# Experts in pairs: both down-projections side by side, one combine per pair

## The reference

```
logits = t @ w_router + b_router            # 288 x 32 experts
top_v, top_e = lax.top_k(logits, 4); gates = softmax(top_v)
# for every expert e, for the tokens that chose it:
hh = xb @ w1[e] + b1[e]                     # 1024 -> 2048
glu, lin = split(hh); glu = min(glu, 7); lin = clip(lin, -7, 7)
act = glu * sigmoid(1.702 * glu) * (lin + 1)
out = act @ w2[e] + b2[e]                   # 1024 -> 1024
y += gate * out                             # back to each token's row
```

## Time and profile before

| | us |
|---|---|
| median of 3 runs | 1418.36 (1416.41 to 1418.98) |
| profiled execution, span (all that the page gives of it) | 1417.7 |
| TensorE matmuls busy | 1293.6 (91%) |
| TensorE weight loads busy (beside the matmuls) | 632.8 |
| VectorE busy | 508.9 (36%) |
| ScalarE busy | 202.4 (14%) |
| GpSimd busy | 138.0 (10%) |
| up-projections, line 1601 | 452.0 |
| down-projections, line 1631 | 226.8 |
| combines, line 1577 | 196.2 |
| gathers, line 1557 | 74.1 |
| read from memory | 460.84 MB |

### The profile page before, as it was taken

How to read it: one execution, slowest core, us unless ns; L and a number is a source line. 1 busy time by engine, 2 the same in 40 slices (tenths; PEclk the granted TensorE clock), 3 DMA queues, 4 the chain that set the end, 5 groups by cost and what they waited for, 6 DMA issues and landing times.

```text
span 1417.7 us, 18156 instructions
## 1 busy us (share of the span) xinstructions
PE 1293.6 (91%) x6994; PEld 632.8 (45%) x6994; DVE 508.9 (36%) x907; ACT 202.4 (14%) x354; POOL 138.0 (10%) x100
## 2 busy tenths in 40 slices
PE   5999997869499999999999999999999999999995
PEld 4788897748232433333333333333333333333341
DVE  3455888546623132222223132222222232222313
ACT  2332011010310111101011111111110111111012
POOL 6102266611300000000000000000000000000000
PEclk9999998979699999999999999999999999999998
DMA  9632386684689999999999999999999999999940
GB/s 316 199 121 76 119 268 209 226 329 176 243 350 413 386 398 398 393 402 385 415 385 416 382 398 398 383 414 384 413 388 411 387 405 389 386 406 392 417 169 35
DMA packets 123892, 467.05 MB, mean 329 GB/s; under 512 B 7440, under 2 KB 54064, under 8 KB 90864
## 3 DMA queue, kind: packets, MB, share of 16 engines
q1 hardware_dynamic: 116848, 455.37, 81.6%
q0 software_dynamic: 1616, 6.65, 1.5%
q10 hardware_dynamic: 5392, 4.54, 1.0%
HBM read 460.84 MB, written 5.70 MB: 329 GB/s over the span
## 4 chain that ended last, share of the span: by engine, by line
PE 84%; DVE 10%; ACT 2%; issue 2%; DMA 2%; DVEq 0%; SPq 0%; ACTq 0%
PE bank L1601 31%; PE bank L1631 16%; PE bank L1577 11%; PE bank L1256 8%; PE bank L1557 5%; PE bank L1420 4%; PE bank L1408 2%; PE bank L1619 1%; DVE rest L978 1%; ACT rest L719 1%; DVE split L931 1%; DMA ring<-w_in 1%; PE bank L1595 1%; DVE rest L1174 1%; DVE rest L1002 1%
## 5 line engine op out<-in xcount | busy, mean ns | idle before, releaser
L1601 PE MATMUL bank<-ring,rest 128*64 128x512 f32 x2048 | 452.0, 594 | 0.0
L1174 DVE TENSOR_TENSOR rest<-rest,bank 128x512 f32<-128x512 f32 (+1 forms) x198 | 133.8, 682 | 498.4 <-PE bank L1577 498.3
L1601 PEld LDWEIGHTS bank<-ring,rest 128*64 128x64 f32 x2048 | 144.3, 137 | 286.9 <-issue 281.2
L1631 PE MATMUL bank<-ring,rest 128*64 128x512 f32 x1024 | 226.8, 595 | 11.1 <-ACT rest L719 11.1
L1577 PE MATMUL bank<-rest 128*128 128x512 f32 (+1 forms) x396 | 196.2, 617 | 24.8 <-DVE rest L1174 23.7
L1256 PE MATMUL bank<-rest,ring 128*128 128x288 f32 (+1 forms) x512 | 125.2, 405 | 16.2 <-DMA ring<-w_in 16.2
L1631 PEld LDWEIGHTS bank<-ring,rest 128*64 128x64 f32 x1024 | 70.7, 137 | 146.6 <-issue 127.9
L1577 PEld LDWEIGHTS bank<-rest 128*128 128x128 f32 (+1 forms) x396 | 51.3, 161 | 166.4 <-DVE rest L1174 97.5
L1256 PEld LDWEIGHTS bank<-rest,ring 128*128 128x128 f32 x512 | 98.0, 193 | 40.9 <-DMA ring<-w_in 16.2
L715 ACT ACTIVATE rest<-rest 128x512 f32<-128x512 f32 x32 | 20.1, 630 | 575.1 <-DVE rest L1192 575.1
L1420 PE MATMUL bank<-split 128*128 128x288 f32 x576 | 86.8, 314 | 10.2 <-DVE split L980 5.7
(11 more groups left out here) (296 smaller groups left out, 779.2 us busy)
## 6 DMA issues: line engine op xcount, KB each, us to landing
ring<-w SPq DMA_DIRECT2D x384, 1024.0 KB, 8.4
ring<-w_in SPq DMA_DIRECT2D x12, 1024.0 KB, 13.4
ring<-k_t SPq DMA_DIRECT2D x8, 1024.0 KB, 5.4
ring<-v_c SPq DMA_DIRECT2D x8, 1024.0 KB, 12.8
ring<-w_xk SPq DMA_DIRECT2D x4, 1024.0 KB, 5.1
ring<-w_xv SPq DMA_DIRECT2D x4, 1024.0 KB, 5.1
ring<-w_out SPq DMA_DIRECT2D x4, 1024.0 KB, 5.9
ring<-w_xq SPq DMA_DIRECT2D x4, 1024.0 KB, 5.8
```

What stands on the lines that cost most here:

```text
L1174: v.tensor_tensor(dst, dst, ps[6 + q % 2][0:R, :], ALU.add).then_inc(comb_free, 1)
L1601: last = t.matmul(out, slots[:, k, :], w[:, col], start=False, stop=(k == KT - 1))
L1631: last = t.matmul(ps[2 + ds][CAP * cg:CAP * cg + CAP, :], actT[:, a * P + CAP * cg:a * P + CAP * cg + CAP], w[:, cg, 512 * ds:512 * ds + 5 ...
```

## The change

Experts are worked in pairs, and the loop's body is two pairs instead of four experts. The code changes in five places.
- A pair's units come as 8 of the first expert's `w1`, 8 of the second's, then the 8 of `w2` in turn from both.
- TensorE does the first up-projection, with the previous pair's combine after unit 3, then the second, with the first expert's transposes after unit 4, then the gather for the next pair, the second expert's transposes and both down-projections. In these the upper 64 partitions of a bank belong to the first expert and the lower to the second, and each half adds up the whole sum over 1024.
- One combine serves a pair: slots 0 to 63 are the first expert's, 64 to 127 the second's.
- The slot weights are no longer built per tile and transposed. The gates are split into three bf16 parts and transposed once, ahead of the loop (`gate_rows`, 96 rows), and the places likewise (`place_rows`). Two bf16 matmuls per pair copy the rows of the two experts to 64 partitions each (banks 6 and 7); ScalarE copies the gates to SBUF, and one VectorE operation writes the gate where the place is the slot's number (`slot_no`).
- The first combine now has 96 rows: three gate parts, with `b2` loaded three times.

```diff
-            q -= W1_UNITS
+            if q < 2 * W1_UNITS:
+                e, q = e + q // W1_UNITS, q % W1_UNITS
...
+            e, q = e + q % 2, (q - 2 * W1_UNITS) // 2
...
 # ScalarE, per pair
+                    act_e.wait_ge(actt_ps, 2 * n + 1)
+                    a.copy(actT[0], ps[4][:, :]).then_inc(actt_done, 1)
+                    act_e.wait_ge(bcast_ps, n + 1)
+                    a.copy(gate_b, ps[6][:, 0:T]).then_inc(gate_copied, 1)
...
+                    evac_gather(n + 2, (j + 1) % 2)
+                    act_e.wait_ge(actt_ps, 2 * n + 2)
+                    a.copy(actT[1], ps[6][:, :]).then_inc(actt_done, 1)
...
 # VectorE, ahead of the loop
+            link(v.tensor_copy(g_part, gates))
+            link(v.tensor_copy(gates3[:, :, 0, :], g_part))
+            link(v.tensor_tensor(g_rest, gates, gates3[:, :, 0, :], ALU.subtract))
...
 # VectorE, per pair
+                    pick_pair(e + 2, (j + 1) % 2)
+                    dve.wait_ge(xg_ps, 2 * n + 2)
+                    select_pair(e + 2)
+                    add_combined(n + r)
+                    activate(2 * n, n * PAIR_UNITS + W1_UNITS, 2 * j)
+                    dve.wait_ge(bcast_ps, n + 1)
+                    dve.wait_ge(gate_copied, n + 1)
+                    v.scalar_tensor_tensor(selGT[:, 0:T], ps[7][:, 0:T], slot_no, gate_b,
+                                           ALU.is_equal, ALU.mult).then_inc(selgt_done, 1)
+                    activate(2 * n + 1, n * PAIR_UNITS + 2 * W1_UNITS, 2 - 2 * j)
...
 # TensorE, per pair
+                    up_bias(1)
+                    for k in range(KT):
+                        up(1, k)
+                        if k == 4:
+                            pe.wait_ge(act_done, 2 * n + 1)
+                            turned(4)
...
+                            t.matmul(ps[6][:, 0:T], oh[j][0:96, :], gate_rows[0:96], start=True, stop=True)
+                            t.matmul(ps[7][:, 0:T], oh[j][0:96, :], place_rows[0:96], start=True, stop=True).then_inc(bcast_ps, 1)
+                    pe.wait_ge(sel_done, n + 2)
+                    pe.wait_ge(actt_done, 2 * n + 1)
+                    gather()
+                    pe.wait_ge(act_done, 2 * n + 2)
+                    pe.wait_ge(selgt_done, n + r + 2)
+                    turned(6)
+                    pe.wait_ge(actt_done, 2 * n + 2)
+                    for q in range(W2_UNITS):
...
+                                for x in range(2):
+                                    last = t.matmul(ps[2 * j + ds][CAP * x:CAP * x + CAP, :],
+                                                    actT[x][:, q * P + CAP * h:q * P + CAP * h + CAP],
+                                                    w[x][:, h, 512 * ds:512 * ds + 512],
+                                                    start=(q == 0 and h == 0), stop=(q == W2_UNITS - 1 and h == 1))
```

More of the change, by code:

```diff
@@ L123, in hybrid_decoder_step @@
         tri, ones_b = C.take(P // 2).bitcast(BF16), C.take(P // 2).bitcast(BF16)
-        iota_slot = C.take(P)
+        iota_slot = C.take(CAP)
+        slot_no = C.take(1)
         iota_e = C.take(NE)
@@ L141, in hybrid_decoder_step @@
         gates = C.take(TT * NE, TT, NE)
+        gate_parts = C.take(TT * NE // 2).bitcast(BF16).rearrange("p (t e) -> p t e", t=TT)
         place = C.take(TT * (NE + 2), TT, NE + 2)
@@ L364, in turn @@
             def turn(i, g, first=0):
-                for j in range(first, BODY * EXP_UNITS):
-                    sp.wait_ge(units_used, g * (BODY * EXP_UNITS) + j - SLOTS + 1)
-                    load_expert_unit(sp, i * BODY, j)
+                for j in range(first, TURN_UNITS):
+                    sp.wait_ge(units_used, g * TURN_UNITS + j - SLOTS + 1)
+                    load_expert_unit(sp, i * (2 * BODY), j)
             for u in range(U_XO - PRE, U_XO):
@@ L540, in _ @@
             pool.wait_ge(outp_done, 2)
-            pool.dma_start(outp[0:NE], b2).then_inc(b2_in, 16)
+            for k in range(3):
+                pool.dma_start(outp[NE * k:NE * k + NE], b2).then_inc(b2_in, 16)
             pool.wait_ge(h_tok, TT)
@@ L1139, in select_pair, with pick_pair @@
                 last.then_inc(sel_done, 1)
-            def pick_bias(e, parity):
-                v.tensor_scalar(oh[parity][0:96], ones[0:96, 0:CAP], pick_e[0:96, bass.ds(e, 1)], None,
-                                ALU.mult).then_inc(oh_done, 1)
+            def pick_pair(e, parity):
+                for half in range(2):
+                    last = v.tensor_scalar(oh[parity][0:96, CAP * half:CAP * half + CAP], ones[0:96, 0:CAP],
+                                           pick_e[0:96, bass.ds(e + half, 1)], None, ALU.mult)
+                last.then_inc(oh_done, 1)
             select_pair(0)
-            pick_bias(0, 0)
+            pick_pair(0, 0)
             for tt in range(TT):
@@ L1174, in add_combined, with activate @@
                     v.tensor_tensor(dst, dst, ps[6 + q % 2][0:R, :], ALU.add).then_inc(comb_free, 1)
+            def activate(x, units, bank):
+                dve.wait_ge(units_used, units)
+                v.tensor_scalar(glu, ps[bank][:, :], LIMIT, None, ALU.min).then_inc(glu_done, 1)
+                v.tensor_scalar(lin, ps[bank + 1][:, :], LIMIT, -LIMIT, ALU.min, ALU.max).then_inc(lin_done, 1)
+                dve.wait_ge(glu_done, x + 1)
+                dve.wait_ge(lin_done, 2 * x + 1)
+                v.scalar_tensor_tensor(lin, lin, 1.0, glu, ALU.add, ALU.mult).then_inc(lin_done, 1)
+                dve.wait_ge(lin_done, 2 * x + 2)
+                dve.wait_ge(sig_done, x + 1)
+                v.tensor_tensor(act, lin, sig, ALU.mult).then_inc(act_done, 1)
@@ L1176, in turn @@
             def turn(i, g, r):
                 for j in range(BODY):
[L1178 to L1201, removed]
+                    n, e = g * BODY + j, i * (2 * BODY) + 2 * j
@@ L1206, in last_combine, with next_places @@
                 dve.wait_ge(comb_free, 2 * TT * (g * BODY + r + 1) + 2)
-            def next_places():
-                v.tensor_scalar(place, place, -float(CAP), None, ALU.add).then_inc(round_step, 1)
+            def next_places(r):
+                v.tensor_scalar(place, place, -float(CAP), None, ALU.add)
+                dve.wait_ge(round_step, r + 2)
+                v.tensor_scalar(place_rows[0:NE], place_f[0:NE], -float(CAP), float(P), ALU.add, ALU.min).then_inc(rows_done, 1)
+                v.tensor_scalar(place_f[0:NE], place_f[0:NE], -float(CAP), None, ALU.add).then_inc(round_step, 1)
             with dve.Fori(0, TURNS) as i:
@@ L1568, in _ @@
             for tt in range(TT):
-                last = t.transpose(ps[7][0:NE, tt * P:(tt + 1) * P], gates[:, tt, :], ident)
-            last.then_inc(gt_ps, 1)
+                R = ROWS[tt]
+                t.transpose(ps[7][0:3 * NE, tt * P:tt * P + R], gates3[0:R, tt].rearrange("p s e -> p (s e)"), ident[0:R, 0:R])
+                last = t.transpose(ps[6][0:NE, tt * P:tt * P + R], place[0:R, tt, 0:NE], ident[0:R, 0:R])
+            last.then_inc(rows_ps, 1)
             def combine(c, pieces=range(2 * TT)):
@@ L1582, in turn, with unit @@
                     n = g * BODY + j
[L1583 to L1587, removed]
+                    def unit(u):
+                        s, fill = (PAIR_UNITS * j + u + PRE) % SLOTS, (PAIR_UNITS * j + u) // SLOTS
+                        pe.wait_ge(ring_in[s], (TURN_UNITS // SLOTS * g + (fills(s) + fill + 1)) * 16)
@@ L1588, in expert_unit, with up_parts, up_bias @@
                         return slot[s]
+                    def up_parts(x):
+                        bank = 2 * j if x == 0 else 2 - 2 * j
+                        return [(ps[bank + q // 2][CAP * (q % 2):CAP * (q % 2) + CAP, :], slice(512 * q, 512 * q + 512))
+                                for q in range(4)]
+                    def up_bias(x):
+                        for out, col in up_parts(x):
+                            t.matmul(out, oh[j][0:96, CAP * x:CAP * x + CAP], b1s[0:96, col], start=True, stop=False)
@@ new lines, in up, with turned @@
+                    def up(x, k):
+                        w = unit(W1_UNITS * x + k)
+                        for out, col in up_parts(x):
+                            last = t.matmul(out, xg[j][:, k, CAP * x:CAP * x + CAP], w[:, col],
+                                            start=False, stop=(k == KT - 1))
+                        last.then_inc(units_used, 1)
+                    def turned(bank):
+                        for a in range(4):
+                            last = t.transpose(ps[bank][:, a * P:(a + 1) * P], act[:, a * P:(a + 1) * P], ident)
+                        last.then_inc(actt_ps, 1)
@@ L1592, in turn @@
                     pe.wait_ge(oh_done, n + 1)
-                    parts = [(ps[q // 2][CAP * (q % 2):CAP * (q % 2) + CAP, :], slice(512 * q, 512 * q + 512)) for q in range(4)]
-                    for out, col in parts:
```

(27 more changed lines are left out.)

89 lines of the change are left out of this document (53 added, 36 removed).

## The result

The changed kernel takes 1340.93 us (median, 1340.22 to 1341.11) against 1417.38 beside it on the same chip. The ratio is 0.9457, with a 95% interval of 0.9441 to 0.9474. The profiled execution took 1340.22 us, with a span of 1338.5.

The account below looks back on a forecast made before the run. TensorE bounds the kernel with loads close behind; afterwards loads set the end. First issue 386.5 + gap 2.6 + loads 916.3, then announcement and last units to 1311.1, + tail 20.4 + 0.7 = 1332.2 us; range 1310 to 1368.

Parts of the forecast that it names:

- TensorE's pair falls to 54.9 us: Expert loop, per pair on TensorE: 63.37 less 7.49 (one combine), 0.66 (wait behind gather) and 0.37 (transposes) gives 54.9 us.
- The new waits have cover: Expert loop: waits for VectorE's weights and ScalarE's copies hide under up-projection units; three units, 5.1 us, for about 1.2 us.
- Then the loads are late: Expert loop: loads need 59.8 us per pair against TensorE's 54.9, so 4.9 us of waits per pair, pieces under 0.9.
- The steps ahead of the loop are hidden: Before the loop: gate splitting (2.1 us) and two further b2 loads end under the first gather, which lasts until 382.9.
- the first issue: Loop start: the 17th load, first after the full ring of 16, issued at 386.5 instead of 385.74.
- 2.49 us per load: Loop: mean of w1 loads at 2.46 and w2 at 2.56 us; 368 loads take 916.3 us.
- gap at the start and announcement of the last load: First pair: 2.6 us of dry load queue, once; loop end: last load announced about 2.2 us after its transfer.
- the tail: From the loop's end to the span's end: 20.0 us as before plus two short VectorE operations, 20.4 us.
- the loads' ceiling: Rival, expert loop: loads themselves cannot exceed 397 GB/s, 2.64 us per load, time 1388 us; chance 0.13.
- TensorE did not stay the bound: Rival, expert loop: TensorE stays the bound because loads can run at 458 GB/s, time 1284 us; chance 0.04.
- The clock did not fall: Rival, units behind each combine and gather: load waits drop TensorE's clock to 0.50, time 1503 us; chance 0.04.
- The side-by-side halves overlap: Rival, down-projections: array halves with two experts no longer overlap, 28.4 instead of 14.2 us per pair, about 1511; chance 0.02.

## Why the prediction was right

It said 1332.2 and the measured time is 8.7 us above it, within the range. The mechanism is the one forecast, step by step, with some sizes off.
- *TensorE's pair falls to 54.9 us*: 54.37. The odd expert's combine, the wait behind the gather and the second set of transposes went as worked out. The transposes in the second up-projection with the two bf16 matmuls take 0.59 + 0.12 + 0.12 = 0.83 (taken as 0.9), the wait ahead of the down-projection 1.1 to 1.2 (taken as 1.33), the 64 down-projection instructions 13.95 (14.18).
- *The new waits have cover*: no matmul waits for VectorE in the loop, and ScalarE's copies cost 0.7 per pair.
- *Then the loads are late*: shown by the cut loads, which free 67 us. The waits begin in the fifth pair (the sixth was forecast) and lengthen a pair by 5.9 us (4.9). Single ones are up to 1.8 us, where pieces of under 0.9 were forecast: in the down-projections TensorE waits for two units at once.
- *The steps ahead of the loop are hidden*: the loop starts at 380.41, before even 383.35. The other kernels with the changed prelude start between 379.1 and 382.7, and the kernel before with its loads cut at 380.6, so those 3 us are no effect of the change.

The sum's terms, forecast and measured: the first issue 386.5, measured 382.79 (-3.7); 2.49 us per load, measured 60.24 / 24 = 2.51, over 368 loads (+7.4); gap at the start and announcement of the last load 2.6 + 2.2, measured 1314.57 - 382.79 - 923.7 = 8.1 (+3.3); the last two units, 1314.57 to 1318.38, 3.8 (+0.3); the tail 20.1 (-0.3); what lies around the span, 2.4 to the median (+1.7). Together +8.7. The first of these follows the loop's start, which varies by 3 us from run to run; that it cancels part of the others is luck.

The term that was mis-sized most is the load: I took 426 GB/s for `w1` from the best four-us windows of the earlier trace rows, and over a long stretch these rows hold 422, as the kernel with 8 KB rows throughout shows. Windows picked at the peak of a rate that swings are an upper bound and no mean.

The rivals: the loads' ceiling was not 397 GB/s; the dips of before were TensorE's, as the earlier trace rows had it, and they are gone. TensorE did not stay the bound beyond the first pairs. The clock did not fall: gaps of up to 1.8 us and a TensorE busy 86% of a stretch left it at 1.00. The rule of the Trainium skill on the clock ("TensorE: Matmul & The Clock Gate", HAM oscillation) did not come true with gaps of this size; the waits in that section's example are longer, and no run here has such. The side-by-side halves overlap with two experts as they did with two parts of one sum (13.95 us for 64 instructions). The 358 GB/s of the Trainium skill ("SBUF — State Buffer", Summary: rules for kernel authors) are passed by a sixth over 600 us.

## What to carry to other kernels

When work is taken off the engine that sets the pace, work out what the transfers need over the whole loop before counting the gain: here 144 us less of TensorE brought 76. The loop ends with the later of two sums, all of the engine's work or all of the stream less what the buffer held at the start; the buffer's lead counts once, not per turn. Then look at how the transfers are laid out in memory, as here rows of twice the length, each load in one stretch, gave another 8 us.

## What the runs showed that I had not expected

The loads now wait inside SyncE's queue. Here are the rows of the loads of `w2` and `w1` (how long the issuing took, min/median/max in ns) and the page's row for all loads (the last number is the median from issue to landing in us); first before, where a load of `w2` took 0.38 us to issue:

```profile
L303 SPq DMA_DIRECT2D ring<-w x128: 367/378/715, 247.0 to 1354.4; - x128
...
ring<-w SPq DMA_DIRECT2D x384, 1024.0 KB, 8.4
```

and now:

```profile
L314 SPq DMA_DIRECT2D ring<-w x128: 367/4101/5017, 382.8 to 1293.3; - x128
L312 SPq DMA_DIRECT2D ring<-w x256: 327/1032/6058, 246.4 to 1263.9; - x128
...
ring<-w SPq DMA_DIRECT2D x384, 1024.0 KB, 22.7
```

Issuing a load of `w2` takes 4.1 us in the median and one of `w1` 1.0, and a load lands 22.7 us after it, which at 2.51 us each is an estimated nine loads under way, of the sixteen that the ring has slots for. The rest must wait behind the load whose issuing is not done. It costs nothing here, as the DMA engines are full, but it makes SyncE's queue look like the bound (27% of the chain), which the cut loads refute: with half the bytes and as many issues it was gone.
